# The delta block of a fused forward pass: the group loops reordered on four engines

## The reference

```python
qkv = silu(short_conv(qkv, conv_w))          # 5 taps along the tokens
q, k = l2_norm(q), l2_norm(k)
decay = exp(where(incl, g[:, None] - g[None, :], -inf))
a_mat = where(strict, (k * beta) @ k.T * decay, 0)
u, w  = solve(eye + a_mat, [v * beta, k * beta * exp(g)])
qk    = (q @ k.T) * decay
# scan over the chunks:
v_new = u - w @ state
o     = (q * exp(g)) @ state + qk @ v_new
state = state * exp(g_last) + k_tail.T @ v_new
```

## Time and profile before

| | us |
|---|---|
| median of 3 runs | 3106.0 |
| lowest and highest | 3100.7, 3111.8 |
| the profiled execution's own time | 3102.9 |
| its span in the profile | 3101.3 |
| PE busy | 2936.9 |
| DVE, ACT, POOL busy | 2130.5, 1394.9, 457.1 |

### The profile page before, as it was taken

How to read it: one execution, slowest core, us unless ns; L and a number is a source line. 1 busy time by engine, 2 the same in 40 slices (tenths; PEclk the granted TensorE clock), 3 DMA queues, 4 the chain that set the end, 5 groups by cost and what they waited for, 6 DMA issues and landing times.

```text
span 3101.3 us, 50798 instructions
## 1 busy us (share of the span) xinstructions
PE 2936.9 (95%) x18548; PEld 2526.8 (81%) x18548; DVE 2130.5 (69%) x3193; ACT 1394.9 (45%) x2304; POOL 457.1 (15%) x356
## 2 busy tenths in 40 slices
PE   7897888888999999999999999999999999999998
PEld 4776777677779998877779988799988777899986
DVE  5564746435569974698678954799745987899645
ACT  3553444445436642333456642466522334466422
POOL 0111111218460001000030001300010000300012
PEclk9998989899999999999999999999999999999999
DMA  6120211212322332222223332223232222323322
GB/s 250 50 53 17 52 36 32 55 28 86 118 95 96 107 106 91 86 88 86 89 95 109 108 105 91 90 102 100 98 102 82 95 82 83 108 95 108 101 99 78
DMA packets 97244, 275.09 MB, mean 89 GB/s; under 512 B 35712, under 2 KB 36864, under 8 KB 95760
## 3 DMA queue, kind: packets, MB, share of 16 engines
q1 hardware_dynamic: 94016, 267.89, 26.6%
q10 hardware_dynamic: 2768, 4.25, 0.4%
q0 software_dynamic: 320, 1.05, 0.1%
HBM read 267.88 MB, written 5.28 MB: 88 GB/s over the span
## 4 chain that ended last, share of the span: by engine, by line
PE 85%; DVE 6%; ACT 5%; issue 2%; SPq 1%; DMA 1%; ACTq 0%; DVEq 0%; POOL 0%; POOLq 0%
PE bank L149 16%; PE bank L151 16%; PE bank L150 16%; PE bank L2051 8%; PE bank L2052 8%; PE bank L2053 8%; DVE weights_lo L142 1%; SPq L670 1%; PE bank L1611 1%; ACT weights_hi L137 1%; DVE short_conv L1149 1%; PE bank L2542 1%; PE bank L1695 1%; PE bank L1678 1%; PE bank L1625 1%
## 5 line engine op out<-in xcount | busy, mean ns | idle before, releaser
L142 DVE TENSOR_TENSOR weights_lo<-weights_raw,weights_hi 128x1024 fp32r<-128x1024 f32 (+2 forms) x258 | 397.8, 1542 | 322.5 <-ACT weights_hi L137 318.9
L137 ACT ACTIVATE weights_hi<-weights_raw 128x1024 fp32r<-128x1024 f32 (+2 forms) x250 | 285.2, 1141 | 439.4 <-PE bank L151 432.4
L149 PE MATMUL bank<-x_hi,weights_hi 128*128 128x512 f32 x832 | 337.0, 405 | 4.5 <-DVE x_lo L1941 2.8
L151 PE MATMUL bank<-x_hi,weights_lo 128*128 128x512 f32 x832 | 326.4, 392 | 0.0
L150 PE MATMUL bank<-x_lo,weights_hi 128*128 128x512 f32 x832 | 325.3, 391 | 0.0
L2051 PE MATMUL bank<-sum_hi,block_hi 128*128 128x256 f32 x960 | 270.8, 282 | 5.0 <-ACT bank L2203 3.6
L150 PE MATMUL bank<-hidden_lo,weights_hi 128*128 128x512 f32 x704 | 273.9, 389 | 0.0
L149 PE MATMUL bank<-hidden_hi,weights_hi 128*128 128x512 f32 x704 | 273.9, 389 | 0.0
L151 PE MATMUL bank<-hidden_hi,weights_lo 128*128 128x512 f32 x704 | 273.9, 389 | 0.0
L2052 PE MATMUL bank<-sum_lo,block_hi 128*128 128x256 f32 x960 | 270.2, 281 | 0.0
L2053 PE MATMUL bank<-sum_hi,block_lo 128*128 128x256 f32 x960 | 269.1, 280 | 0.0
(11 more groups left out here) (436 smaller groups left out, 7374.7 us busy)
## 6 DMA issues: line engine op xcount, KB each, us to landing
raw_pair<-w_ff1in SPq DMA_DIRECT2D x42, 1024.0 KB, 4.9
raw_pair<-w_ff2in SPq DMA_DIRECT2D x42, 1024.0 KB, 4.8
weights_raw<-w_mix SPq DMA_DIRECT2D x72, 512.0 KB, 3.5
weights_raw<-w_ff1out SPq DMA_DIRECT2D x32, 704.0 KB, 4.1
weights_raw<-w_ff2out SPq DMA_DIRECT2D x32, 704.0 KB, 4.1
weights_raw<-w_tail SPq DMA_DIRECT2D x42, 512.0 KB, 3.5
mod_weights<-w_mod SPq DMA_DIRECT2D x6, 2048.0 KB, 16.6
weights_raw<-w_dn SPq DMA_DIRECT2D x24, 512.0 KB, 3.7
```

The costliest lines, as they stand in the source:

```text
L137: nc.scalar.activation(K.wh[:, slot, 0:cols], K.raw[:, slot, 0:cols], ACT.Copy).then_inc(S.wh_ready, 1)
L142: nc.vector.tensor_tensor(K.wl[:, slot, 0:cols], K.raw[:, slot, 0:cols], K.wh[:, slot, 0:cols].bitcast(F32), ALU.subtract).then_inc(S.raw_ ...
L149: nc.tensor.matmul(out, K.wh[:, slot, a:b], xh, start=start, stop=False)
L151: return nc.tensor.matmul(out, K.wl[:, slot, a:b], xh, start=False, stop=stop)
```

## The change

- ACT's `decays(t)` comes ahead of `squares(t)`, and PE makes `rows(t)` ahead of `turn_heads(t)`; nothing runs a tile ahead any more. DVE's `norms(t)` stands just before its use.
- The copy of the next group's first slab out of its bank, and the split of a further slab's weights, move from the start of a group to step n = 4 of the scan before (`next_begun`; DVE's half stands behind `new_state(4)`). The next slab's copy, split and middle taps move behind the tile loop.
- DVE takes 8 tap operations instead of 6 after the small inverse, 1 in each level step instead of 2 from step 6 on, and 10 in the scan (3, 3, 2, 2) where there were none. ACT's silus and middle taps move to other steps.
- `state_start` moves from behind the taps of step 17 to step 16, ahead of that step's taps.
- PE takes one part in each tile (two in the first two tiles of group 0, where it was two in every tile of group 0), and 14 later parts in groups 0 to 2 (20, 20 and 16 before). In the scan, the part between `answer` and `renew` goes.
- Head 0's turn in the tail comes one entry later.

```diff
--- before.py
+++ after.py
@@ -427,7 +427,7 @@
 
 SPLIT_AT = {11: 0, 13: 1, 15: 2, 17: 3, 20: 4, 22: 5, 24: 6, 26: 7}
 
-NORMED = {TAIL.index(("u", m)) + 1: m for m in range(8)}
+NORMED = {TAIL.index(("u", m)) + (1 if m else 2): m for m in range(8)}
 GATED = {TAIL.index(("w", n)): tuple(range(8 + 4 * n, 12 + 4 * n)) for n in range(2)}
 GATED.update({i: GATED.get(i, ()) + (m,) for i, m in NORMED.items()})
 GATE_ORDER = tuple(y for i, entry in LATE for y in GATED.get(i, ()))
@@ -825,6 +825,14 @@
         act_head(act, 0, 5)
         act_sum_rows(act)
 
+    def next_begun(act, G):
+
+        if G + 1 < GROUPS:
+            act_raw(act, G + 1, 0, True)
+        else:
+            act_gate(act, 0, True)
+        split_hi(act, DN_SLAB + 6 * G + 8, 0, 1024)
+
     def act_group(act, G):
         more = G + 1 < GROUPS
 
@@ -853,26 +861,18 @@
                 last = nc.scalar.activation(K.decs[t % 2][:, c, :], pb[4][:, 128 * c:128 * c + 128], ACT.Exp,
                                             bias=K.ncum[:, t, at:at + 1])
             last.then_inc(S.dec_ready, 1)
-        if more:
-            act_raw(act, G + 1, 0, True)
-        else:
-            act_gate(act, 0, True)
-            split_hi(act, s, 0, 1024)
-            act_gate(act, 1)
-        squares(0)
-        if more:
-            split_hi(act, s, 0, 1024)
-            act_center(act, G + 1, 0)
         if G == 0:
+            next_begun(act, 0)
             act.wait_ge(S.gate_step, GATE_STEPS)
         for t in range(TILES):
-            if t + 1 < TILES:
-                squares(t + 1)
             decays(t)
-            if t == 3 and more:
-                act_raw(act, G + 1, 1)
+            squares(t)
         if more:
+            act_raw(act, G + 1, 1)
+            act_center(act, G + 1, 0)
             act_center(act, G + 1, 1)
+        else:
+            act_gate(act, 1)
         act.wait_ge(S.dve_step, (NORM_STEPS + SMALL_STEPS) * G + 2 * TILES)
         nc.scalar.activation(K.knorm[:, :, :], K.ssq[:, :, 0:2], ACT.Sqrt).then_inc(S.knorm_ready, 1)
         act.wait_ge(S.bt_ready, TILES * G + TILES + CREDIT)
@@ -941,10 +941,10 @@
                 renewed(0, i - STEPS_INNER - 3)
             if i == 3:
                 split_hi(act, DN_SLAB + 6 * G + 13 if more else TAIL_SLAB + 9, 1, 1024)
-            if more and i in (2, 8, 12):
-                head = {2: 1, 8: 2, 12: 3}[i]
-                act_head(act, G + 1, head)
-                act_center(act, G + 1, head + 2)
+            if more and i in (0, 12, 16):
+                act_head(act, G + 1, {0: 1, 12: 2, 16: 3}[i])
+            if more and i in (1, 13, 17):
+                act_center(act, G + 1, {1: 3, 13: 4, 17: 5}[i])
         for n, (f, b, x) in enumerate(scan_steps()):
             if n == 0:
                 continue
@@ -952,8 +952,11 @@
             renewed(n, 1)
             if x is not None:
                 state_out(x, (f, b))
-            if more and n in (2, 4):
-                act_head(act, G + 1, 3 + n // 2)
+            if more and n == 3:
+                act_head(act, G + 1, 4)
+            if more and n == 4:
+                next_begun(act, G + 1)
+                act_head(act, G + 1, 5)
 
     def ctx_bank(G, i):
         return pb[2 + i % 2 if G == 0 else 2][:, 0:CTX]
@@ -1193,16 +1196,14 @@
                                                      in1=wide(pb[5 + t % 2][:, 128 * j:128 * j + 128], 1, 2),
                                                      op0=ALU.mult, op1=ALU.mult)
             ins.then_inc(S.bt_ready, 1)
-        norms(0)
-        split_lo(dve, s, 0, 1024)
+        if G == 0:
+            split_lo(dve, s, 0, 1024)
         for t in range(TILES):
-            if t + 1 < TILES:
-                norms(t + 1)
+            norms(t)
             if t < 4:
                 scores(t)
             system(t)
-            if t == 4:
-                split_lo(dve, s + 1, 1, 1024)
+        split_lo(dve, s + 1, 1, 1024)
         nc.vector.tensor_tensor(K.tail2[:, :, :].rearrange("p t (d j) -> p t d j", j=2),
                                 K.tail_s[:, :, :].rearrange("p t (d h) -> p t d h", h=HEADS)[:, :, :, 2 * G:2 * G + 2],
                                 wide(K.n2[:, :, :], 2, 2), ALU.mult).then_inc(S.tail_ready, 1)
@@ -1243,7 +1244,7 @@
         if more:
             split_lo(dve, s + 3, 1, 1024)
             split_lo(dve, s + 4, 0, 1024)
-            take(conv, 6)
+            take(conv, 8)
         else:
             split_lo(dve, s + 5, 1, 1024)
         def state_start():
@@ -1264,12 +1265,13 @@
                     x = K.e[own, 2 * d:2 * d + 2, t, other]
                     ins = nc.vector.tensor_tensor(x, x, pb[5 + i % 2][own, 0:128].rearrange("p (j v) -> p j v", v=64), ALU.subtract)
             ins.then_inc(S.e_ready, 1)
-            take(conv, 1 if i < STEPS_FIRST else 2)
+            if i == STEPS_LEVEL - 2:
+                state_start()
+            take(conv, 1)
             if i in (2, 5) and not more:
                 split_lo(dve, s + 6 + i // 5, i // 5, 1024)
             if i == 5 and more:
                 split_lo(dve, s + 5, 1, 1024)
-        state_start()
 
         def residual(n, tiles):
 
@@ -1316,6 +1318,9 @@
                 out_sum(*before)
             if n < 5:
                 new_state(n, (f, b))
+                take(conv, 3 if n < 3 else 2)
+            if n == 4 and more:
+                split_lo(dve, s + 6, 0, 1024)
             before = (x, (f, b)) if x is not None else None
         out_sum(*before)
         take(conv, 99)
@@ -1546,7 +1551,7 @@
 
     def pe_group(pe, G, fills):
         s, v = DN_SLAB + 6 * (G + 1), DN_EVIC + 6 * (G + 1)
-        fill, later = fills[G], islice(fills[G + 1], 20 if G + 2 < GROUPS else 16)
+        fill, later = fills[G], islice(fills[G + 1], 14 if G + 1 < GROUPS else 16)
         if G == 0:
             take(fill, 8)
             pe_sum_rows(pe)
@@ -1649,15 +1654,11 @@
                     last = nc.tensor.matmul(pb[5 + i % 2][own, 64 * j:64 * j + 64], K.pp[other, i % 2, 64 * j:64 * j + 64],
                                             K.e[other, 2 * d + j, TILE_ORDER[i % TILES], other], start=True, stop=True)
             last.then_inc(S.w_ready, 1)
-        turn_heads(0)
-        rows(0)
-        products(0)
         for t in range(TILES):
-            take(fill, 1 if G else 2)
-            if t + 1 < TILES:
-                turn_heads(t + 1)
-                rows(t + 1)
-                products(t + 1)
+            rows(t)
+            turn_heads(t)
+            products(t)
+            take(fill, 2 if G == 0 and t < 2 else 1)
         take(fill, 99)
         busy(pe, pb[turn_bank(0)], 8)
         for i in range(3):
@@ -1738,9 +1739,10 @@
             tiles = (f, b)
             for d, t in enumerate(tiles):
                 against(n, d, t)
-            if x is not None:
+            if x is None:
+                take(later, 1)
+            else:
                 answer(n, x, tiles)
-            take(later, 1)
             if n == 1:
                 pe.wait_ge(S.e_ready, STEPS_LEVEL * (G + 1) + CREDIT)
             for d, t in enumerate(tiles):
```

## The result

The changed kernel takes 3003.6 us (median of 4 runs, 3002.0 to 3007.0) against 3105.2 for the kernel before (4 runs, 3100.7 to 3111.8): a ratio of 0.967, 95% interval 0.965 to 0.969. The profiled executions differ by just 100.0 us of span, 3101.3 to 3001.3. The direction and most of the size came as argued, and about 18 us more came than the sum of 81.7 had.

What follows compares the result with a forecast made beforehand. PE, busy 2936.9 of 3101.3 us, was taken as the bound, so gains come only from its waits and low clock. Terms 79.7 + 6 + 12 - 13 + 4 - 6 - 2 + 1 = 81.7 us gave 3024, range 3004 to 3065.

Steps and rivals of the forecast that it cites:

- tile loops, less the moved parts: Tile loops: new order removes PE's waits and low clock; loops of 18.5 and 19.9 us, 79.7 us saved in four groups.
- clock behind the loop: Start of the fill: 3.0 us at the lower clock level cost 1.5 us, four times; 6 us back.
- state copies and taps in the scan: Scan of groups 0 to 2: earlier state copies save net 12 us, taps delaying the residual cost 13.
- level steps ("smaller terms"): Level steps: corrections no longer delayed by silu and middle tap in one step; 4 us saved.
- low clocks, DVE, POOL, the inverse: Costs: clock falls in half of seven places, -6; DVE sharing with POOL and the inverse's way through DRAM, -2.
- tail, and the start of the block: Tail's start: head 0's turn no longer holds PE, but ACT's bank copy does; 1 us saved, not 8.
- The table load: Tile 0: ACT's exponential table load of 1.28 us costs 0.4 to 0.5 us at `rows(1)`, 0.25 at the next turn.
- 4 of the 5.6 us: Level steps: of 5.6 us PE waits in three corrections behind ACT, 4 go once silu and middle tap are separated.
- The allowances: Costs set aside: -6 for low clocks from new waits, -2 for DVE beside POOL and a late inverse.
- wait of the loop stayed: Rival, tile loop: half of the 42.8 us of waits and of the low clock stay; 3065 us, chance 0.14.
- the rival of a low clock without waits: Tile loop: clock stays low although nothing waits; gain of 10 us, chance 0.07.
- The rival of the scan: Scan: recurring waits of 0.7 to 1.9 us hold the clock low, 88 us lost; 3130 us, chance 0.04.

Runs made afterwards that it cites:

- The four kernels of the level steps: Silu and middle tap in different steps or together, with one DVE tap a step (3003.6, 3006.5 us) or two from step 6 (3005.5, 3011.1 us).
- a_old_taps: Changed kernel with taps, silus and middle taps at their old places and no taps in the scan: 3011.1 us, ratio 0.970.
- a_state_late: Changed kernel with the state copies back behind the taps of level step 17: 3008.4 us, ratio 0.969.
- a_old_normed: Changed kernel with head 0's turn in the tail one entry earlier, as before: 2998.8 us, ratio 0.967.

## Why the prediction was right, and where it was not

| term | predicted, us | seen |
|---|---|---|
| tile loops, less the moved parts | 79.7 | 81.5 - 2.1 = 79.4 |
| clock behind the loop | 6 | 17 parts of 0.7 came in, the fills grew by 6.5: 11.9 - 6.5 = 5.4 |
| state copies and taps in the scan | 12 - 13 = -1 | 12.0 - 14 parts of 0.7 = 2.2 |
| level steps ("smaller terms") | 4 | 14.2 |
| low clocks, DVE, POOL, the inverse | -6 - 2 = -8 | nothing beside the lengths of the loops and scans |
| tail, and the start of the block | 1 | -1.2 |
| sum | 81.7 | 100.0 |

**The tile loop** was right in mechanism and size. The working gave 18.6 and 17.2 us without waits; the loops at full clock are 19.0 and 17.6 with PE never idle. The 1.3 us of waits that I allowed for each did not come; in two loops 1.7 and 2.2 us of low clock came instead, so the sum agrees partly by luck. The table load, which I had priced at up to 0.75 us a loop, did not hold PE up: in groups 1 to 3 it no longer stands in the loop but ends while PE makes the first `rows`, and in group 0, where it still does (123.29 to 124.57, the first exponential from 124.58), the loop has no wait for the exponentials either. From the start of the load to the first exponential are 1.29 us there and 1.30 before, with 1.28 of loading.

**The step that failed** is the term "4 of the 5.6 us" for the level steps: they gave 14.2 us. The mechanism (silu and middle tap in one step delay a correction) was right and is half of it; the other half, DVE's second tap, was not in the sum. The time lies below the range for the same reason: the range's lower end is the forecast with all costs at nothing, and the level steps had no upper bound of their own. (The costs add up to 13 + 6 + 2 = 21, which I called some 20; with 21 the end would be 3003. But the costs were not nothing, as the next paragraphs show, so that would have been luck.) I took the price of the pair of silu and taps from one row, PE's wait at L1643 behind L911, and left the rest of the stage unpriced. The trace of before had all of it: the windows of its level steps, first group 1, then group 3, which has no convolution to do, and PE's waits in group 1 that I had not priced:

```profile
338.50:376.60 38.10, 33.71 (x585) 27.29 (x583) 30.38 (x56) 24.64 (x57) 1.15 (x1) 1.00 0.08 28
627.10:660.90 33.80, 33.00 (x585) 27.09 (x584) 13.20 (x24) 20.23 (x51) 0.00 (x0) 1.00 0.11 34
```

```profile
PE bank L1649 <- ACT product L914: 0.9, 1, 0.9
PE bank L1643 <- ACT product L914: 0.5, 1, 0.5
```

Group 3 does the same 585 matmuls in 33.8 us. The difference of 4.3 us is what the convolution costs there; twice 4.3 and 5.6 of group 0 make the 14.2. Of the 4.3 the row behind L911 is 1.9, two waits behind L914 are 1.4, and some 1 us lies in gaps too short for a row and in matmuls shown longer. The four kernels of the level steps then showed both halves: about 2 us of ACT's pair, about 2.3 of DVE's second tap.

**The scan** was over-priced, but by less than its rows of waits suggest. In steps 2 to 5 I had 0.95, 0.7, 0.7 and 1.9 us, 4.25 in a group; the steps are 0.98, 0.39, 0.39 and 1.43 longer than in `a_old_taps`, 3.2 in a group, so 9.6 stand for the 13. In step 3 the residual starts 1.36 us behind the end of the new state (337.17 to 338.53) instead of 0.66, so 0.7 later where I had 0.9 to 1.2, and part of that lies under `answer`. At `inner` the waits are 1.7 us where they were 1.1. The state copies and what hangs on them then have 2.2 + 9.6 = 11.8 us by difference, near the 12 predicted; `a_state_late` shows 6.1 us of waits for them directly, less than 10.7 since one tap a step stands ahead of them and no longer two. At step 1 the wait is 0.5 us, where I had 1.2.

**The allowances** of 8 us are the second part of what the sum missed: low clocks came at two of the seven places, and are in the loops' 19.3 and 19.8 us and the scan's 32.1. In the profile of `a_old_normed`, the same instructions in the delta block, there are none: the scans are 31.5 us three times and the loops 17.6. DVE and POOL held nothing up, and PE came to the turned inverse with no wait of more than 0.2 us. The 7.0 us at the tail's start are the 6.9 that I had from the times of before.

**The rivals.** No wait of the loop stayed, and no scan lost its clock but for the last 1.3 us of group 2's: the scan of group 1 is at 1.00 through waits of 0.5, 0.6 and 1.2 us. Two loops ran at 1.00 from end to end, with 32 transposes among the 102 small matmuls of one (240 to 257.6). No run shows the 10 us that the prediction gives the rival of a low clock without waits; in their place the runs showed loops of 19.0 and 17.6 us at 1.00. Against this rival I had said that a third of the matmuls of the level steps are transposes. That is their share of PE's busy time; by number they are 72 of 585 in group 1. The rival of the scan adds 21 us for the next loops in its text and 18 in its sum; neither came.

**What stays open**: why the clock fell behind two scans of one profile and behind none of another with the same instructions there. It cost 1.7 us the first time, and 2.2 in the loop and some 0.6 in the scan the second.

## What to carry to other kernels

A stage that runs several times is its own control: set the instance that lacks the neighbour's work beside the ones that have it, and the difference is the price, small gaps included; the rows of waits leave out gaps too short for a row. When one engine's queue is at the head of a chain, serve first what PE must have next, and put PE's independent work where it stands and not beside it: with one part of each step moved from behind `renew` to ahead of it, the scan held one part more and was 2.2 us shorter in each group. Independent work is worth most where something is late: with 20 parts taken early, the fill was short of cover for ACT's copies and, in one group, for the inverse's way through DRAM.

## What the runs showed of the hardware

**A wait cost twice, and the second half could be bought back.** Dummy matmuls in PE's waits made the kernel before 28 us faster (clock of the loops 0.90 to 1.00 for 0.73 to 0.79), and gave 4.0 us in two waits of the tail, of 7.0 and 4.6 us.

**A small DVE operation stood as long as POOL's instruction beside it.** The same operation in tile 2 of group 0 and in tile 1 of group 1 of the changed kernel, and POOL's mask beside the latter:

```profile
133.37 0.17 DVE L1175 TENSOR_SCALAR head_squares<-head_squares 128x4 f32<-128x4 f32 x1
...
246.74 1.51 POOL L1828 TENSOR_TENSOR level_part<-system,level_mask 64x256 f32<-64x256 f32 x2 [2.41 <-DVE system L1194]
246.88 0.61 DVE L1175 TENSOR_SCALAR head_squares<-head_squares 128x4 f32<-128x4 f32 x1
```

It ends at 247.49, and so does the first of POOL's two equal instructions, 246.74 + 0.75. In the kernel before, 20 of the 24 such operations of the block took 0.17 us; the other four, beside POOL's clearing of the inverse, took 1.1 to 2.1 and ended with it (415.26 + 2.06 = 417.32 and 414.64 + 2.66 = 417.30). It cost nothing here, as DVE was not what PE waited for.
